# The delta rule's triangular inverse moved from behind the input projection to among its last four chunks

## The reference, cut to what matters

```python
z = jnp.matmul(h, w_in).astype(f32)                 # the input projection
...
q_b = _l2norm(heads(q_b)) * HEAD_DIM ** -0.5        # x * rsqrt(sum(x * x) + EPS)
k_b = _l2norm(heads(k_b))
...
# gated delta rule
ratio = jnp.exp(jnp.where(causal, gc[..., :, None] - gc[..., None, :], -jnp.inf))
kk = jnp.where(strict, jnp.einsum('bhncd,bhnsd->bhncs', k, k) * ratio, 0.0)
a_mat = jnp.eye(c) + beta[..., None] * kk
u_v = triangular_solve(a_mat, beta[..., None] * v, ...)
w_k = triangular_solve(a_mat, (beta * gamma)[..., None] * k, ...)
qk = jnp.einsum('bhncd,bhnsd->bhncs', q, k) * ratio
u = uv_n - jnp.einsum('bhcd,bhdv->bhcv', w_n, state)         # per chunk of tokens
o = einsum(qg_n, state) + einsum(qk_n, u)
...
# gated linear attention: decays per channel, so the scores need a product for every pair of positions
scores = jnp.einsum('bhcd,bhsd,bhcsd->bhcs', q_n, k_n, decay)
```

## Time and profile before

| | |
|---|---|
| median of 3 runs | 2091.34 us (2090.42 to 2091.6) |
| the profiled execution | 2086.85 us |
| its span in the trace | 2085.0 us |
| PE busy | 2022.3 us (97%) |
| DVE busy | 1238.4 us (59%) |
| ACT busy | 810.9 us (39%) |
| inverse, first Y product to start of `u0` | 123.42 to 151.61 us |
| running steps on DVE, start to start of `out`'s copy | 151.18 to 176.14 us |
| granted TensorE clock over the whole run | 0.995 |

### The profile page before, as it was taken

How to read it: one execution, slowest core, us unless ns; L and a number is a source line. 1 busy time by engine, 2 the same in 40 slices (tenths; PEclk the granted TensorE clock), 3 DMA queues, 4 the chain that set the end, 5 groups by cost and what they waited for, 6 DMA issues and landing times.

```text
span 2085.0 us, 30554 instructions
## 1 busy us (share of the span) xinstructions
PE 2022.3 (97%) x13049; PEld 1776.0 (85%) x13050; DVE 1238.4 (59%) x1682; ACT 810.9 (39%) x1027; POOL 225.0 (11%) x185
## 2 busy tenths in 40 slices
PE   8988999999999999999999999999999999999998
PEld 7975998999888888889888888888888888878998
DVE  8878555777544655354554555545767744755454
ACT  6533455655522222243342222234222223455444
POOL 1000001413111001100101001110100111001011
PEclk9999999999999999999999999999999999999999
DMA  7425545454643453332233354333545533304553
GB/s 265 162 102 196 210 162 205 158 195 164 228 164 109 164 194 133 118 123 81 81 110 141 129 190 159 134 119 123 190 177 188 192 118 115 127 21 164 184 179 110
DMA packets 54152, 317.04 MB, mean 152 GB/s; under 512 B 6016, under 2 KB 12416, under 8 KB 23808
## 3 DMA queue, kind: packets, MB, share of 16 engines
q1 hardware_dynamic: 50864, 308.99, 41.9%
q10 hardware_dynamic: 3152, 6.10, 0.9%
HBM read 314.01 MB, written 1.05 MB: 151 GB/s over the span
## 4 chain that ended last, share of the span: by engine, by line
PE 82%; DVE 9%; ACT 5%; issue 3%; DMA 0%; SPq 0%; DVEq 0%; ACTq 0%
PE psum L272 26%; PE psum L274 25%; PE psum L273 25%; ACT w_hi L253 3%; DVE w_lo L261 2%; PE psum L1373 1%; PE psum L1356 1%; PE psum L1779 1%; DVE normed_lo L1955 0%; DMA raw<-in_w_in_r 0%; DVE xc L1566 0%; DVE work L462 0%; PE psum L1384 0%; PE psum L971 0%; DVE work L1949 0%
## 5 line engine op out<-in xcount | busy, mean ns | idle before, releaser
L272 PE MATMUL psum<-normed_hi,w_hi 128*128 128x256 f32 (+1 forms) x2248 | 757.5, 337 | 13.0 <-DVE normed_lo L1955 7.4
L273 PE MATMUL psum<-normed_lo,w_hi 128*128 128x256 f32 (+1 forms) x2248 | 747.9, 333 | 0.0
L274 PE MATMUL psum<-normed_hi,w_lo 128*128 128x256 f32 (+1 forms) x2248 | 747.7, 333 | 0.0
L261 DVE TENSOR_TENSOR w_lo<-raw,w_hi 128x2048 fp32r<-128x2048 f32 (+2 forms) x246 | 509.9, 2074 | 368.7 <-ACT w_hi L253 368.0
L253 ACT ACTIVATE w_hi<-raw 128x2048 fp32r<-128x2048 f32 (+2 forms) x246 | 421.9, 1715 | 176.2 <-PE psum L274 172.3
L272 PEld LDWEIGHTS psum<-normed_hi,w_hi 128*128 128x128 f32 x2248 | 424.0, 189 | 62.2 <-issue 11.6
L273 PEld LDWEIGHTS psum<-normed_lo,w_hi 128*128 128x128 f32 x2248 | 424.3, 189 | 43.3 <-issue 1.2
L274 PEld LDWEIGHTS psum<-normed_hi,w_lo 128*128 128x128 f32 x2248 | 424.0, 189 | 42.4
L272 PE MATMUL psum<-h_hi,w_hi 128*128 128x256 f32 (+1 forms) x1265 | 410.1, 324 | 6.6 <-DVE w_lo L261 2.2
L273 PE MATMUL psum<-h_lo,w_hi 128*128 128x256 f32 (+1 forms) x1265 | 407.7, 322 | 0.0
L274 PE MATMUL psum<-h_hi,w_lo 128*128 128x256 f32 (+1 forms) x1265 | 407.6, 322 | 0.0
(11 more groups left out here) (386 smaller groups left out, 1345.7 us busy)
## 6 DMA issues: line engine op xcount, KB each, us to landing
raw<-in_mod SPq DMA_DIRECT2D x72, 1024.0 KB, 4.8
raw<-in_a_up SPq DMA_DIRECT2D x42, 1024.0 KB, 4.7
raw<-in_b_up SPq DMA_DIRECT2D x42, 1024.0 KB, 4.7
raw<-in_ffn_up SPq DMA_DIRECT2D x22, 1024.0 KB, 4.8
raw<-in_a_down SPq DMA_DIRECT2D x32, 704.0 KB, 4.0
raw<-in_b_down SPq DMA_DIRECT2D x32, 704.0 KB, 4.0
raw<-in_ffn_down SPq DMA_DIRECT2D x16, 704.0 KB, 4.0
raw<-in_wo SPq DMA_DIRECT2D x8, 1024.0 KB, 4.7
```

Of the source, the lines that this page charges most:

```text
L261: dve.tensor_tensor(w_lo[:, slot, 0:size], raw[:, raw_slot(("main", g)), 0:size], w_hi[:, slot, 0:size].bitcast(F32), ALU.subtract).then_i ...
L272: pe.matmul(out, lh, rh, start=first, stop=False, skip_group_check=group)
L273: pe.matmul(out, lh, rl, start=False, stop=False, skip_group_check=group)
L274: return pe.matmul(out, ll, rh, start=False, stop=last, skip_group_check=group)
```

## The change

The inverse's six levels now stand among the 32 k-tiles of the four `w_in_g` chunks on TensorE (`gates(n)` issues the next n k-tiles), in PSUM banks 3, 4, 5 and 7 in place of 0 to 3. In a level TensorE's list is: Y of group 0, one k-tile, Y of group 1, two k-tiles, X of group 0, X of group 1, two k-tiles. The reciprocal root is computed on ACT straight from PSUM (`delta_act_root`, which replaces DVE's `delta_dve_sums`) with two DVE steps left of the Newton step; the decay ratio's minimum moves into eight `tensor_scalar` in `delta_dve_difference`; the identity that the inverse starts from is written by ACT; "kk" and "tokens" stand in the middle of `w_in_b` 4, at its sixth k-tile; and DVE's multiplications are put in another order. DVE's `split_lo` 14, 15 and 16 and the evacuations of `w_in_g` 0 to 2 stand within levels. Running steps 0 to 3 come earlier on DVE and 0 to 2 on TensorE; `split_lo` 17 comes later, behind the copy of `u0`. All steps of the chain from `u0` on keep their work.

```diff
+        def delta_act_root(act, o):
+            need(act, "gdn_pe", "sums")
+            o(act.activation(sq4, two_banks(3, T), ACT.Abs_reciprocal_sqrt, scale=-1.0, bias=col("eps")), "guess")
+            o(act.activation(half_sq, sq4, ACT.Square, scale=0.5 ** 0.5), "half")
...
+        def delta_act_identity(act):
+            need(act, "gdn_dve", "unit")
+            for r in BLOCKS:
+                act.activation(work[r, 0:1024].rearrange("p (n t) -> p n t", t=HD),
+                               ident[r, r].unsqueeze(1).to_broadcast([HD, 16, HD]), ACT.Copy).then_inc(level_x, 1)
...
-            gc8 = small[:, cols["gcol"]:cols["gcol"] + 8].unsqueeze(2).to_broadcast([P, 8, P])
-            o(dve.tensor_tensor(RT, two_banks(5), gc8, ALU.subtract), "difference")
+            for n in range(2):
+                for h in range(HEADS):
+                    mm = dve.tensor_scalar(RT[:, 4 * n + h, :], two_banks(5)[:, 4 * n + h, :], gcol[:, n, h:h + 1], 0.0, ALU.subtract, ALU.min)
+            o(mm, "difference")
...
+            need(dve, "gdn_act", "half")
+            o(dve.scalar_tensor_tensor(half_sq, two_banks(3, T), -EPS, half_sq, ALU.add, ALU.mult))
+            o(dve.scalar_tensor_tensor(sq4, half_sq, 1.5, sq4, ALU.add, ALU.mult))
...
+        def delta_dve_strict(dve, o):
+            need(dve, "gdn_act", "ratio")
+            o(dve.tensor_tensor(BR, BR, RT, ALU.mult), "key_decays")
+            need(dve, "gdn_pe", "kk")
+            for n in range(2):
+                o(dve.tensor_tensor(by_parity(NT, n), psum[:, 3:5, n * T:(n + 1) * T].rearrange("p a (b t) -> p a b t", t=P),
+                                    by_parity(BR, n), ALU.mult), "strict" if n else None)
...
+        def delta_dve_scores(dve, o):
+            o(dve.tensor_tensor(RT, RT, triu[:, :].unsqueeze(1).to_broadcast([P, 8, P]), ALU.mult), "causal")
+            need(dve, "gdn_pe", "qk")
+            for n in range(2):
+                o(dve.tensor_tensor(by_parity(QT, n), psum[:, 5:7, n * T:(n + 1) * T].rearrange("p a (b t) -> p a b t", t=P),
+                                    by_parity(RT, n), ALU.mult), "scores" if n else None)
...
+        def inverse_dve(dve, i, between=None):
+            for a in range(2):
+                dve.wait_ge(level_pe, i * 8 + 2 * (a + 1))
+                dve.tensor_tensor(YB[a], psum[:, 3 + 4 * a, 0:T].rearrange("p (n t) -> p n t", t=HD),
+                                  second_half[:, i:i + 1, :].to_broadcast([P, 4, HD]), ALU.mult).then_inc(level_y, 1)
+            if between is not None:
+                between()
+            for a in range(2):
+                dve.wait_ge(level_pe, i * 8 + 2 * (a + 3))
+                dve.tensor_tensor(XX[a], XX[a], bank(4 + a).rearrange("p (s n t) -> p s n t", s=2, t=HD), ALU.subtract).then_inc(level_x, 1)
...
+        def inverse_pe(pe, i, gates, before_x=None):
+            inverse_pe_y(pe, i, 0)
+            gates(1)
+            inverse_pe_y(pe, i, 1)
+            gates(2)
+            if before_x is not None:
+                before_x()
+            inverse_pe_x(pe, i, 0)
+            inverse_pe_x(pe, i, 1)
...
+        def gates_pe(pe):
+            tile = 0
+            def more(n):
+                nonlocal tile
+                for _ in range(n):
+                    c, k = divmod(tile, KT)
+                    s = Step(jobs["w_in_g"], c)
+                    if k == 0:
+                        bank_free(pe, s)
+                        pe.wait_ge(lo_ready, s.g + 1)
+                    for n_ in range(2):
+                        w = slice((n_ * KT + k) * P, (n_ * KT + k + 1) * P)
+                        mm = three_passes(pe, psum[:, s.slot, n_ * T:(n_ + 1) * T], (w_hi[:, s.slot, w], w_lo[:, s.slot, w]),
+                                          (xs_hi[:, k, X], xs_lo[:, k, X]), k == 0 and n_ == 0, k == KT - 1, group=True)
+                    if k == KT - 1:
+                        mm.then_inc(chunk_done, 1)
+                    tile += 1
+            return more
...
             win_pe(pe, "w_in_b", 2, midway=lambda: delta_pe_spread(pe, delta_order), at=2)
-            win_pe(pe, "w_in_b", 3)
+            win_pe(pe, "w_in_b", 3, midway=lambda: gated_pe_key(pe, gated_order), at=6)
             delta_pe_sums(pe, delta_order)
-            win_pe(pe, "w_in_b", 4)
-            win_pe(pe, "w_in_g", 0)
-            win_pe(pe, "w_in_g", 1, midway=lambda: delta_pe_tokens(pe, delta_order), at=2)
-            delta_pe_products(pe, delta_order, lambda: gated_order(
-                pe.matmul(psum[:, 7, 0:T], gk_up[64:80, :], zs[64:80, :], start=True, stop=True), "gk"))
-            win_pe(pe, "w_in_g", 2)
-            win_pe(pe, "w_in_g", 3)
-            delta_pe(pe, delta_order)
+            def keys():
+                delta_pe_keys(pe, delta_order)
+                delta_pe_tokens(pe, delta_order)
+            win_pe(pe, "w_in_b", 4, midway=keys, at=5)
+            gates = gates_pe(pe)
+            gates(2)
+            delta_pe_queries(pe, delta_order)
+            need(pe, "gdn_dve", "strict")
+            need(pe, "gat_act", "u")
+            inverse_pe(pe, 0, gates, lambda: need(pe, "gdn_dve", "scores"))
+            gates(2)
+            inverse_pe(pe, 1, gates)
+            gates(2)
+            inverse_pe(pe, 2, gates)
+            gates(2)
+            inverse_pe(pe, 3, gates)
+            gates(2)
+            inverse_pe(pe, 4, gates)
+            gates(2)
             run_pe_clear(pe)
+            inverse_pe(pe, 5, gates)
+            run_pe_step(pe, 0)
+            gates(2)
+            inverse_pe_lower(pe)
+            run_pe_step(pe, 1)
+            mods_pe(pe, 1)
+            inverse_pe_end(pe)
+            run_pe_step(pe, 2)
             mods_pe(pe, 1)
             delta_pe_u0(pe, delta_order)
-            run_pe_step(pe, 0)
-            run_pe_step(pe, 1)
+            run_pe_step(pe, 3)
+            run_pe_step(pe, 4)
             delta_pe_state(pe, delta_order)
-            run_pe_step(pe, 2)
+            run_pe_step(pe, 5)
             gated_pe_tokens(pe, gated_order)
-            run_pe_step(pe, 3)
+            run_pe_step(pe, 6)
             delta_pe_w(pe, delta_order)
-            run_pe_step(pe, 4)
+            run_pe_step(pe, 7)
             mods_pe(pe, 1)
-            run_pe_step(pe, 5)
+            run_pe_step(pe, 8)
             delta_pe_u1(pe, delta_order)
-            run_pe_step(pe, 6)
+            run_pe_step(pe, 9)
             mods_pe(pe, 1)
-            run_pe_step(pe, 7)
             delta_pe_out(pe, delta_order, 0)
-            run_pe_step(pe, 8)
-            run_pe_step(pe, 9)
-            delta_pe_out(pe, delta_order, 1)
             run_pe_step(pe, 10)
             run_pe_step(pe, 11)
+            delta_pe_out(pe, delta_order, 1)
+            run_pe_step(pe, 12)
             delta_pe_out(pe, delta_order, 2)
-            run_pe_step(pe, 12)
             run_pe_step(pe, 13)
             delta_pe_out(pe, delta_order, 3)
             run_pe_step(pe, 14)
...
             delta_act_squares(act, delta_order)
+            delta_act_root(act, delta_order)
             split_hi(act, 12)
             delta_act_decays(act, delta_order)
+            delta_act_identity(act)
             split_hi(act, 13)
-            delta_act_rsqrt(act, delta_order)
+            gated_order = order(act, "gat_act")
+            gated_act_first(act, gated_order)
             split_hi(act, 14)
-            delta_act_ratio(act, delta_order)
+            gated_act_logs(act, gated_order)
             split_hi(act, 15)
             split_hi(act, 16)
+            gated_act_decays(act, gated_order)
             split_hi(act, 17)
-            gated_order = order(act, "gat_act")
-            gated_act_first(act, gated_order)
             mod_scalar(act)
-            gated_act_decays(act, gated_order)
             delta_act_spread(act)
+            gated_act_gates(act, gated_order)
...
+            win_evac(dve, "w_in_b", 3)
+            dve.wait_ge(evacuated, jobs["w_in_b"].base + 3)
+            gated_order(dve.tensor_copy(U3[:, 1:3, :], z[:, DF:DF + 2, :]), "u")
+            delta_dve_unit(dve, delta_order)
             split_lo(dve, 12)
-            win_evac(dve, "w_in_b", 3)
+            delta_dve_strict(dve, delta_order)
+            delta_dve_tokens(dve, delta_order)
+            win_evac(dve, "w_in_b", 4)
             split_lo(dve, 13)
-            delta_dve_sums(dve, delta_order)
-            win_evac(dve, "w_in_b", 4)
-            split_lo(dve, 14)
-            delta_dve_unit(dve, delta_order)
-            win_evac(dve, "w_in_g", 0)
-            split_lo(dve, 15)
-            delta_dve_tokens(dve, delta_order)
-            win_evac(dve, "w_in_g", 1)
-            split_lo(dve, 16)
-            delta_dve_start(dve, delta_order)
+            delta_dve_scores(dve, delta_order)
+            inverse_dve(dve, 0, lambda: delta_dve_weights(dve, delta_order))
+            inverse_dve(dve, 1, lambda: split_lo(dve, 14))
+            def gates_first():
```

(32 more changed lines are left out.)

141 lines of the change are left out of this document (54 added, 87 removed).

## The result

The changed kernel takes 2099.47 us (median of 5 runs, 2097.26 to 2099.73) against 2091.34 us (5 runs on the same chip, 2090.1 to 2093.41). The ratio is 1.0042, with a 95% interval of 1.0031 to 1.0053: slower by 0.4%.

What follows compares the result with a forecast made beforehand. Three limits: TensorE, then TensorE-DVE ping-pong in the inverse, then DVE's running steps. -3.2 us to `u0` and +8.4 behind gave +5.2; +4.6 was taken, 2095.9 us, range 2087.5 to 2100.5.

Steps and rivals of the forecast that it cites:

- The first half: From "sums" through the levels to `u0`: `u0` at 148.4 in place of 151.6, a gain of 3.2 us.
- A: The forecast itself: lists out of step, half clock, +4.6 us, own range 2094.3 to 2097.8; chance 0.45.
- So 0.1 in 16 such places, 1.5: In the levels: going over from other matmuls to a k-tile costs 0.1 us in each of 16 places.
- Rival D: Going over costs 0.3 us more in 16 places, as behind "sums": +4.8 on top, 2100.7 us; chance 0.12.
- The lower bound, going over free: Changes between matmul shapes in the levels cost nothing, making the whole +3.7 us in place of +5.2.
- From "sums" to the first X: Ahead of the levels: table load on the path, "unit" at 94.0, TensorE waiting 4 us, first X at 106.3.
- Levels bound by TensorE, DVE hidden: Between Y and the next Y, DVE's 3.8 us lie beside TensorE's 4.7, with 0.9 to spare.
- The clock: Behind `u0`, TensorE's waits of 3.3 and 2.3 us bring half clock: 0.8 and 1.6 us more.
- Rival C: DVE does not wait for `s1`, `w` and `u1`: whole -2.8 us (2088.5), or -4.3 with going over free; chance 0.2.
- three-part sum: Behind `u0` at full clock, TensorE's new list adds 1.2 us for `s1`, 2.0 for `w`, 2.4 for `u1`.
- Rival B: The clock stays full behind the new waits: +2.2 us, 2093.5; chance 0.23.
- 10 us are left for it, so it is there: The third filler input, loaded after split 17 ends at about 152.3, arrives before its use at about 162.

## Why the prediction was right or wrong

The sign was right, and so was the mechanism behind `u0` (lists out of step, DVE waiting for `s1`, `w` and `u1`, half clock). The first half was wrong in its sign: 3.2 us were to be gained up to `u0`, and 1.0 was lost. The median was 3.6 us above the forecast of 2095.9 and 1.7 above A's own range; it lies in the full range (2087.5 to 2100.5), but near its end. By the trace the sum was 5.1 us short (10.3 against 5.2): the first X 0.7, the levels 3.7, the part behind `u0` 0.9, and 0.2 back between `lower` and `u0`. Another 0.6 went by taking 4.6 in place of 5.2. That the profiled run of before lay 4.5 us below its median, and that of after only 2.2, gave 2.3 back. This is luck: with 4.5 for both the median would have been 2101.8, outside the range.

- **"So 0.1 in 16 such places, 1.5" is the step that failed.** The price of going over was read from one place, between two matmuls of the k-tile itself, and left out the seams on both sides. It is 0.34 to 0.38 us for a visit, by the rows and by the runs with two and four visits: 3.8 to 4.5 us more than forecast in 16. `lower` came at 148.0 adjusted and not 143.6, of which 0.7 was there at the first X. Rival D had about this price, and its 2100.7 us was the closest, but it had it from a first matmul of 0.68 us, and here the first takes 0.38: the rest lies in the seams around it. D had the size right and the place wrong. The lower bound, going over free, was of no use: nothing in the earlier trace rows was at zero, and moving towards it made the forecast 0.6 us worse.
- **From "sums" to the first X** the chain held: "unit" at 94.5 adjusted for 94.0, with the table's load on it. The half clock of "tokens" behind the new wait was not in it. The Trainium skill's page "ScalarE: Activation LUTs", section "What ACT_TABLE_LOAD costs", has 1380 ns of draining on top; here the activation starts 0.02 us behind the load, and taking the switch off the path gave 1.35 us and not 2.66.
- **Levels bound by TensorE, DVE hidden**: right.
- **`s1`, `w`, `u1`.** At full clock 1.2 + 2.0 + 2.4 = 5.6 us was forecast; 1.09 + 2.06 + 2.06 = 5.2 us are there when the clock is held. The three-part sum was right, though the price of the list as such is 4.9 us by the traces at full clock (4.3 by the medians, 5.9 by the ratios): with the new list DVE has no small waits for running steps, with the old places 0.43 and 0.19 us are back.
- **The clock** was forecast at 2.4 us, and is 8.9 - 5.2 = 3.7 us in the profile, and 3.3 and 5.1 in the medians of the two kernels with zeros (2.7 and 3.8 by the ratios). The forecast let it fall twice, for step 4 and `s1` and for step 7, the filler and part of step 8; it stayed at the 1.2 GHz level over the turns and the steps around them too. Rival B, a full clock, is refuted. The Trainium skill's "TensorE: Matmul & The Clock Gate", "HAM oscillation — how this bites in real kernels", has it that each burst between waits starts cold and that the cure is to order the work so that the engine stays warm; the run with zeros in the waits agrees, with a granted clock of 1.00 there and 3.3 us.
- **Split 17** was charged 2.2 us on DVE, and is 2.29 there. But it makes TensorE's wait of 3.1 us, with the low clock right behind it, and in a faster list it makes the filler's data late: 4.5 to 7.7 us. Taking it away does not keep the clock up in the new list: it falls one step later. "10 us are left for it, so it is there" held for the changed kernel only because TensorE was late itself.
- **Rival C** was refuted as it named it: TensorE's step and product were longer than DVE's next step in all three places.

## What to carry to other kernels

Moving a waiting chain in among other work wins its waits and pays for each seam: count how often the engine changes from one kind of product to the other, price a change by both its edges, and group the visits until a wait of the other engine comes back. Ahead of a product that another engine waits for, put nothing that needs that engine's next step; a long piece of work on that engine in this place, such as a split, delays for its own time and makes the other one wait, with the low clock behind the wait. And before the new order is given up, undo its parts one at a time: here the kernel that keeps the inverse among the chunks and moves five other things is 7 us faster than before, and two misplaced items, the split and TensorE's running steps, cost 12.
